# A third block of up to 64 tokens joins the first in a small pair, in the expert loop of a mixer and MoE block

## The reference

```python
logits = (t @ w_router + b_router).astype(jnp.float32)
top_vals, top_idx = lax.top_k(logits, TOP_K)
gate = jax.nn.softmax(top_vals, axis=-1)
...
h = xb @ w_up[e] + b_up[e]
g = jnp.minimum(h[:, :D_FF], SWIGLU_LIMIT)
lin = jnp.clip(h[:, D_FF:], -SWIGLU_LIMIT, SWIGLU_LIMIT)
act = g * jax.nn.sigmoid(SWIGLU_ALPHA * g) * (lin + 1.0)
return act @ w_down[e] + b_down[e]
```

## Time and profile before

| | us |
|---|---|
| time before, median of 3 runs | 2248.12 (2245.98 to 2250.63) |
| span of the profiled execution, first to last instruction | 2239.1 |
| TensorE busy | 2147.8 (96%) |
| VectorE busy | 1606.1 (72%) |
| ScalarE busy | 1206.7 (54%) |
| GpSimd busy | 559.1 (25%) |

### The profile page before, as it was taken

How to read it: one execution, slowest core, us unless ns; L and a number is a source line. 1 busy time by engine, 2 the same in 40 slices (tenths; PEclk the granted TensorE clock), 3 DMA queues, 4 the chain that set the end, 5 groups by cost and what they waited for, 6 DMA issues and landing times.

```text
span 2239.1 us, 32629 instructions
## 1 busy us (share of the span) xinstructions
PE 2147.8 (96%) x10498; PEld 1784.5 (80%) x10499; DVE 1606.1 (72%) x1842; ACT 1206.7 (54%) x1239; POOL 559.1 (25%) x519
## 2 busy tenths in 40 slices
PE   7999988997899999999999999999999999999996
PEld 7887987685687888888888888888888888888885
DVE  4788876458855656787588675977975787677766
ACT  4422261331744545566476565757754676565755
POOL 1001031115301112124044041414411252121313
PEclk9999999997999999999999999999999999999998
DMA  7224276413966766889599695979986799778877
GB/s 185 64 79 142 81 163 205 167 67 138 360 218 218 229 212 220 305 282 353 184 363 369 231 324 181 376 268 302 369 289 213 250 365 328 226 246 295 296 248 270
DMA packets 287302, 541.65 MB, mean 242 GB/s; under 512 B 37302, under 2 KB 53798, under 8 KB 286146
## 3 DMA queue, kind: packets, MB, share of 16 engines
q1 hardware_dynamic: 262866, 495.07, 63.7%
q0 software_dynamic: 24368, 45.72, 8.1%
HBM read 513.61 MB, written 65.13 MB: 258 GB/s over the span
## 4 chain that ended last, share of the span: by engine, by line
PE 58%; issue 6%; DVE 6%; ACT 3%; DMA 2%; DVEq 0%; ACTq 0%; POOL 0%; SPq 0%; POOLq 0%
PE ex_ps_l L2927 8%; PE ex_ps_l L2926 8%; PE ex_ps_g L2926 7%; PE ex_ps_g L2927 7%; PE ex_ps_y L2926 5%; PE ex_ps_y L2927 5%; PE ex_ps_g L2930 4%; PE ex_ps_l L2930 4%; PE ex_ps_y L2930 3%; DVE ex_w_lo L2693 3%; PE ex_ps_t L2864 2%; ACT ex_w_hi L2561 2%; PE ex_ps_t L2874 2%; PE ex_ps_l L2881 1%; PE ex_ps_g L2936 1%
## 5 line engine op out<-in xcount | busy, mean ns | idle before, releaser
L2693 DVE TENSOR_TENSOR ex_w_lo<-ex_late,ex_w_hi 128x2048 fp32r<-128x2048 f32 x204 | 464.0, 2289 | 230.9 <-ACT ex_w_hi L2561 166.9
L2401 POOL TENSOR_TENSOR ex_passed<-keep_ident 128x1 f32<-128x1 f32 x136 | 137.0, 1007 | 1153.3 <-ACT ex_y L2604 1126.5
L2561 ACT CAST ex_w_hi<-ex_late 128x2048 fp32r<-128x2048 f32 x170 | 324.6, 1909 | 129.4 <-PE ex_ps_g L2927 62.8
L2693 DVE TENSOR_TENSOR ex_w_lo<-keep_sig_o,ex_w_hi 128x2048 fp32r<-128x2048 f32 x136 | 310.1, 2291 | 111.1 <-ACT ex_w_hi L2561 111.1
L2561 ACT CAST ex_w_hi<-keep_sig_o 128x2048 fp32r<-128x2048 f32 x134 | 255.2, 1905 | 136.0 <-PE ex_ps_g L2927 39.1
L2926 PE MATMUL ex_ps_g<-ex_w_hi,ex_x_hi 128*128 128x512 f32 x784 | 308.2, 393 | 3.3 <-DVE ex_w_lo L2693 1.8
L2926 PE MATMUL ex_ps_l<-ex_w_hi,ex_x_hi 128*128 128x512 f32 x784 | 308.9, 394 | 1.2 <-DVE ex_w_lo L2693 1.2
L2927 PE MATMUL ex_ps_g<-ex_w_lo,ex_x_hi 128*128 128x512 f32 x784 | 306.6, 391 | 0.0
L2927 PE MATMUL ex_ps_l<-ex_w_lo,ex_x_hi 128*128 128x512 f32 x784 | 305.9, 390 | 0.0
L2926 PE MATMUL ex_ps_y<-ex_w_hi,ex_h_hi 128*128 128x512 f32 x544 | 217.8, 400 | 3.1 <-DVE ex_h_lo L2729 2.5
L2930 PE MATMUL ex_ps_g<-ex_w_hi,ex_x_lo 128*128 128x512 f32 x544 | 212.7, 391 | 0.0
(11 more groups left out here) (502 smaller groups left out, 4081.2 us busy)
## 6 DMA issues: line engine op xcount, KB each, us to landing
keep_sig_o<-in_w_up_dram SPq DMA_DIRECT2D x102, 1024.0 KB, 8.8
ex_late<-in_w_up_dram SPq DMA_DIRECT2D x102, 1024.0 KB, 8.8
ex_late<-in_w_down_dram SPq DMA_DIRECT2D x102, 1024.0 KB, 8.1
keep_weights<-in_w_up_dram SPq DMA_DIRECT2D x68, 1024.0 KB, 8.3
keep_sig_o<-in_w_down_dram SPq DMA_DIRECT2D x34, 1024.0 KB, 8.1
st_tab<-tabs SPq DMA_DIRECT2D x8, 1408.0 KB, 11.8
keep_weights<-in_w_in_dram SPq DMA_DIRECT2D x5, 1024.0 KB, 5.5
pr_late_pieces<-in_w_in_dram SPq DMA_DIRECT2D x5, 1024.0 KB
```

Of the source, the lines that this page charges most:

```text
L2401: pool.tensor_tensor(passed[:, :], ident[:, 0:1], ident[:, 0:1], ALU.add).then_inc(passed_done, 1)
L2561: nc.scalar.copy(w_hi[:, j % SPLIT, :, :], raw(j)).then_inc(hi_done, 1)
L2693: v.tensor_tensor(w_lo[:, j % SPLIT, :, :], raw(j), w_hi[:, j % SPLIT, :, :].bitcast(F32), ALU.subtract).then_inc(lo_done, 1)
```

## The change

An expert with 257 to 320 tokens has a third block of at most 64. It now runs as a small pair made of its first and its third block, and then a single pass with the second one. Before it was a full pair of the first two, and a single pass of the third. For this:

- the plan is computed with three thresholds for each expert (192, 256 and 320 tokens) in place of one, and the bit of the full pair is set where the count is over 192 and not over 256, or over 320;
- `paired(plan)` replaces `plan & 1` in the index of the single pass, since a small pair can now stand ahead of it;
- `gather` and `scatter` copy their two columns one by one, since they need not be neighbours any more, and GpSimd loads the next expert's plan in every pass to know which column the second block is in.

```diff
-        over_at = sb("over_at", [1, E], F32)
+        over_at = sb("over_at", [1, 3, E], F32)
...
-                pool.memset(over_at[:, 0:E - 1], float(P + SMALL)).then_inc(consts_set, 1)
-                pool.memset(over_at[:, E - 1:E], float(P)).then_inc(consts_set, 1)
+                for w in range(3):
+                    pool.memset(over_at[:, w, 0:E - 1], float((P + SMALL, 2 * P, 2 * P + SMALL)[w])).then_inc(consts_set, 1)
+                pool.memset(over_at[:, :, E - 1:E], float(P)).then_inc(consts_set, 1)
...
-                    step(v.tensor_tensor(over[:, :], cnt_f[:, :], over_at[:, :], ALU.is_gt))
+                    step(v.tensor_tensor(overs[:, :, :], cnt_f[:, :].unsqueeze(1).to_broadcast([1, 3, E]), over_at[:, :, :], ALU.is_gt))
...
+                    step(v.tensor_tensor(over_1[:, :], overs[:, 0, :], overs[:, 1, :], ALU.subtract))
...
+                    step(v.tensor_tensor(over[:, :], over_1[:, :], overs[:, 2, :], ALU.add))
...
             with eng.If((plan & 2) > 0):
-                body(n + (plan & 1), e, 1, plan)
+                body(n + paired(plan), e, 1, plan)
...
+        def paired(plan):
+            return (plan | (plan >> 2)) & 1
+
+        def three_blocks(plan):
+            return (plan >> 1) & paired(plan)
...
-                def gather(n, at, turn):
-
-                    pool.tensor_copy(gather_at[:, :], places[:, bass.ds(at, PAIR), 0:1].rearrange("p b o -> p (b o)")).then_inc(gather_set, 1)
+                def gather(n, at, second, turn):
+
+                    pool.tensor_copy(gather_at[:, 0:1], places[:, bass.ds(at, 1), 0:1].rearrange("p b o -> p (b o)"))
+                    pool.tensor_copy(gather_at[:, 1:2], places[:, bass.ds(second, 1), 0:1].rearrange("p b o -> p (b o)")).then_inc(gather_set, 1)
...
-                    pool.tensor_copy(scatter_at[:, :, :], places[:, bass.ds(at, PAIR), :]).then_inc(scatter_set, 1)
+                    pool.tensor_copy(scatter_at[:, 0:1, :], places[:, bass.ds(at, 1), :])
+                    pool.tensor_copy(scatter_at[:, 1:2, :], places[:, bass.ds(second, 1), :]).then_inc(scatter_set, 1)
...
                     n = pool.snap(n)
-                    own, after = e * COLS, e * COLS + COLS
-                    if blocks == 2:
-                        after = after - single_follows(e, plan) * (COLS - PAIR)
-                    else:
-                        own = own + (plan & 1) * PAIR
+                    follows = single_follows(e, plan) if blocks == 2 and kind is AHEAD else 0
+                    own = pool.snap(e * COLS + (paired(plan) if blocks == 1 else 0))
+                    second = pool.snap(own + three_blocks(plan) + 1)
+                    after = pool.snap(e * COLS + COLS - follows * (COLS - 1))
...
-                        gather(n + 1, pool.snap(after), n * 4 + 3)
+                        if e is LAST_E:
+                            skip = 1
+                        else:
+                            skip = follows | three_blocks(pool.value_load(
+                                keep["plan"][0:1, bass.ds(e + 1, 1)], min_val=1, max_val=8 * 2 * E + 7))
+                        gather(n + 1, after, pool.snap(after + 1 + skip), n * 4 + 3)
...
                 pass_on(None)
-                gather(0, 0, 1)
+                first_plan = pool.value_load(keep["plan"][0:1, 0:1], min_val=1, max_val=8 * 2 * E + 7)
+                gather(0, 0, pool.snap(three_blocks(first_plan) + 1), 1)
```

More of the change, by code:

```diff
@@ L1614, in project_out_route @@
         square = split_q[:, D:D + HALF]
-        two, three, threes, plan_a, plan_b, plan_c, over = (
-            split_q[0:1, 2 * D - (i + 1) * E:2 * D - i * E] for i in range(7))
+        two, three, threes, plan_a, plan_b, plan_c, over, over_1 = (
+            split_q[0:1, 2 * D - (i + 1) * E:2 * D - i * E] for i in range(8))
+        overs = split_q[0:1, 2 * D - 11 * E:2 * D - 8 * E].rearrange("p (w e) -> p w e", w=3)
         weighted = split_q[:, D + HALF:D + HALF + K4 * E].rearrange("p (k e) -> p k e", k=K4)
@@ L1657, in project_out_route @@
         t_t = t_dram.rearrange("(j p) d -> p j d", p=P)
-        CONSTS = 11 + WAVES - 1 + 6
+        CONSTS = 11 + WAVES - 1 + 8
         PLACES_AT = 3
@@ L2412, in gather, with scatter @@
                             bounds_check=last_token, oob_is_err=False).then_inc(x_full[b], 16)
-                def scatter(n, at, turn, blocks):
+                def scatter(n, at, second, turn, blocks):
                     for b in range(PAIR):
@@ L2448, in add_rows, with last_pass @@
                         compute_op=ALU.add).then_inc(y_free[b], 16)
-                def last_pass(n, at, turn, blocks):
+                def last_pass(n, at, second, turn, blocks):
                     for b in range(PAIR):
@@ L2498, in one_pass @@
                         pass_on(n * 4 + 2)
-                        gather(n + 1, pool.snap(after), n * 4 + 3)
+                        if e is LAST_E:
[4 more added lines that the diff above has]
+                        gather(n + 1, after, pool.snap(after + 1 + skip), n * 4 + 3)
                     if kind is LAST:
-                        last_pass(n, pool.snap(own), n * 4 + 2, blocks)
+                        last_pass(n, own, second, n * 4 + 2, blocks)
                     else:
-                        scatter(n, pool.snap(own), n * 4 + 4, blocks)
+                        scatter(n, own, second, n * 4 + 4, blocks)
                 pass_on(None)
-                gather(0, 0, 1)
+                first_plan = pool.value_load(keep["plan"][0:1, 0:1], min_val=1, max_val=8 * 2 * E + 7)
+                gather(0, 0, pool.snap(three_blocks(first_plan) + 1), 1)
                 pool.wait_ge(h3_out, 16 * TT)
@@ L2530, in later @@
                     pass_on(n * 4)
-                    gather(n, at, n * 4 + 1)
-                    scatter(n, at, n * 4 + 2, blocks)
+                    gather(n, at, at + 1, n * 4 + 1)
+                    scatter(n, at, at + 1, n * 4 + 2, blocks)
                     if blocks == 1:
```

## The result

The changed kernel takes 2226.4 us (median of 4 runs, 2225.1 to 2234.0), beside 2247.2 us for the kernel before (4 runs, 2246.0 to 2250.6). The ratio is 0.9907, with a 95% interval of 0.9893 to 0.992. That is 20.8 us less, by this interval 18.0 to 24.0; the sum of the prediction was 19.8 less.

A forecast was written before the change was run, and what follows sets the result against it. TensorE was taken as the bound, busy throughout pairs, so only matmuls count there. −21.8 + 0.4 + 1.0 + 0.4 + 0.2 = −19.8 us took 2248.1 to 2228.3 us; mechanism bounds 2226 to 2236, range with nearest rivals 2224 to 2238.

The forecast's parts named there:

- What is removed: Pairs of experts 9 and 22: 48 low_rows matmuls fewer each, at 0.227 us, so −21.8 us for both.
- The end of the small pair: Handover to the same expert's single pass: most of the 1.27 us of stalls vanish, 0.2 charged per expert, +0.4 us.
- What is added at every single pass: Three register instructions ahead of ScalarE's and VectorE's first operations: 0.2 us, uncovered only behind five small pairs, +1.0 us.
- a window that grows by more than 0.3 us where nothing was changed: Sign of being wrong: windows of passes that the change doesn't touch grow by more than 0.3 us.
- GpSimd: Extra load and copies in each pass: gather's DMAs at most 3.3 us later, within 10.1 us of slack, cost 0.
- Starts: Added work ahead of the very first gather, +0.4 us, and VectorE's extra operations in the router, +0.2 us.
- From span to median: The median stands 9.0 us above the profiled span, and the change has no part outside the span.
- The sum: All terms together: −21.8 + 0.4 + 1.0 + 0.4 + 0.2 = −19.8 us.
- The copies hold VectorE: Rival: two more GpSimd copies in each of 33 passes block VectorE, 12 us, leaving 7.9 us gain: 2240; chance 0.10.
- The weights take over: Rival: shorter pairs with the same 12 MB bring back weight waits of a few us, about 2234; chance 0.03.
- It doesn't do what it says: Rival: the two experts still get a full pair, only the additions are left, +1.6 us: 2250; chance 0.02.
- the gather comes late: Rival: GpSimd's additions exceed the 10.1 us slack, paid in some 33 passes; at 12 us +43 us: 2291; chance 0.04.

The follow-up runs named there:

- plan_reloaded: The changed kernel with one more plan load on every engine at the start of each single pass; ratio to the kernel before 0.9929 (0.9913 to 0.9946).
- round_before_last_y: The changed kernel, with ScalarE rounding chunk 3 of the next pass ahead of its last ex_y; ratio to the kernel before 0.988 (0.9864 to 0.9895).
- all_pairs_small: The changed kernel with experts 1, 4 and 14 also run as small pairs, their results wrong; ratio to the kernel before 0.9832 (0.9796 to 0.9868).
- before_again: The kernel before, unchanged, profiled a second time; span 2249.8 us, device time 2251.65 us.
- gpsimd_eight_more: The changed kernel with eight tiny GpSimd operations ahead of each gather's copies in every pass; ratio to the kernel before 1.0063 (1.0047 to 1.008).

## Why the prediction was right

- **What is removed** (−21.8 us): right. The pairs' windows went to 62.04 and 59.80 us, as forecast, and `low_rows` to 48. The way to cost it, start to start over equal stretches (0.227 us a matmul), held; by duration (0.39 us each) it would have been 37 us. The prediction set the Trainium skill beside it ("TensorE: Matmul & The Clock Gate", "Back-to-back issue gap"): the sustained gap would have given 12.6 us, and the measured 21.4 decides against it for these float32 matmuls.
- **The end of the small pair** (+0.4): right, 10.88 − 10.68 = 0.20 and 10.88 − 10.76 = 0.12 us. With the code moved by 4 expert 9 takes 95.75 us and expert 22 93.52, so the handover to the same expert costs next to nothing. All three runs on the handover support its mechanism: the stall grows with what stands between the passes (`plan_reloaded`, where every engine has the load), goes when ScalarE's rounding alone is taken off that path (`round_before_last_y`), and returns for another expert (`all_pairs_small`).
- **What is added at every single pass** (+1.0): mis-sized; the loops say 2.1 to 2.4, and that is two errors of opposite sign. ScalarE's gap grew by 0.16 us (1.35 to 1.51), where 0.2 was said. In TensorE's time, with the code moved, that is 0.04 to 0.19 a pass, 0.4 to 0.5 us for the five. But the step "behind a single pass or a full pair this is covered" was right only for the registers. It asked what is added and not where the old instructions come to lie: one pair of VectorE instructions got 0.13 us slower in all 17 single passes, +2.2 us, a cost of the change that four unrelated memsets take away. One of the prediction's own signs of being wrong, a window that grows by more than 0.3 us where nothing was changed, was all but met: expert 13's single pass grew by 0.29.
- **GpSimd** (0): right that it costs nothing. In the single passes the gather moved by 0.9 us behind a single one and by 2.4 behind another expert's pair (1 to 3 was said), and by 4.3 for experts 9 and 22 (from 7.1 to 11.4 us behind the mark). The slack was smaller than computed, since the landing time is not fixed at its median of 7.4 us: a gather 8.3 to 8.8 us later already brings waits of 2.2. The rival of the late gather priced it in some 33 passes; at that delay it is seven.
- **Starts** (+0.6): nothing came through in the profiles. The first gather is issued 2.57 us behind GpSimd's first operation of the stage, 1.16 before, so 1.4 us later where 0.9 was said. But from that operation to the first mark it takes 617.66 − 567.85 = 49.8 us after, and 610.68 − 560.03 = 50.7 before (50.1 in `before_again`), and the stretch of the router stage named above takes 29.7 us in `before_again` and after. That the bytes decide there, as the prediction has it, fits, but was not tested.
- **From span to median**: the step "the median stands 9.0 us above the span" was wrong as a reading. The device time of an execution is 1.8 us above its own span (2251.65 and 2249.8 us in `before_again`). The other 7 us were the short first profile. Since the same 9.0 us was added before and after, the difference of 19.8 was not touched by it.
- **The sum.** For the loop alone the terms give −21.8 + 0.4 + 1.0 = −20.4 us, and the loops without expert 2 measure −19.3. The additions cost more than said, and the starts, +0.6, cost nothing that shows. That the total of −19.8 comes so near is in part luck, and the times, with 18.0 to 24.0, could not tell.
- **The rivals.** *The copies hold VectorE*: `ex_w_lo` keeps its 2.29 us, and two more operations in every pass cost nothing. While a GpSimd copy takes 2.26 us, no operation of VectorE comes apart. That the loser of the port pair blocks fully (the Trainium skill, "SBUF — State Buffer", "SBUF: two separate sides") shows here for GpSimd alone. *The weights take over*: no wait for a weight chunk is in the list of TensorE's waits, though the single passes behind the two pairs run at a DMA share of 1.03 to 1.05. *It doesn't do what it says* and *the gather comes late* fell with the windows and the waits.

## What to carry over

A matmul that was taken out of a stretch where TensorE never waits came off the time at its start-to-start distance (0.227 us), not at its duration (0.39), and what a neighbouring engine does between two passes decided how much of it was given back. When a change's rest of 1 or 2 us doesn't fit, compare the same pairs of instructions before and after for their distance: code that is only moved can be slower. Compare loops from mark to mark and not spans, and take a second profile of the kernel before.

## What was not expected of the hardware

- Two VectorE instructions in a row take 0.79 or 0.92 us from start to start by where they lie in the engine's program. Moving them by 4 or by 16 instructions removed the 0.13 us; which places are bad was not mapped, nor what makes them so.
- In the router stage 12 of 13 profiles have one or two pauses of ScalarE of 2.3 to 4.5 us for which the trace names no releasing instruction ("issue" or "remote"), and that stretch takes 6.4 to 7.3 us more than in the one profile that has none. The loop of 1575 us of the kernel before repeats within 0.1, that of the changed kernel within 1.8, which is expert 2's pair.
- The granted clock can fall to its lower level for a few us behind a pause of TensorE of 2 us: behind three of the seven waits of `gpsimd_eight_more` it did, for 1.5 us each on top of the wait, and behind four it did not.
- Eight tiny GpSimd operations (128x1) take 10.45 us beside VectorE's subtractions, 1.3 us each, and 2.64 us in a pair's pass where VectorE is idle:

```profile
1070.74 2.64 POOL L2419 TENSOR_TENSOR ex_spare<-keep_ident 128x1 f32<-128x1 f32 x8
...
1073.82 2.29 DVE L2716 TENSOR_TENSOR ex_w_lo<-ex_late,ex_w_hi 128x2048 fp32r<-128x2048 f32 x1 [4.14 <-ACT ex_w_hi L2584]
```
